# Two more pairs of output-projection tiles by seven block products, on one core

## What is computed

```python
u, gate = proj[..., :E_A], proj[..., E_A:]
pooled = multiscale_causal_pool(u)
y = jnp.einsum('bsgc,gcd->bsgd', pooled, w_grp_a[i]).reshape(b, s, E_A) * scale_a[i]
x = x + (y * jax.nn.silu(gate)) @ w_out_a[i]
...
kv_in = rmsnorm(x, norm_kv)
...
x = x + (merged * jax.nn.silu(gate)) @ w_out_b[i]
return rmsnorm(x, norm_f)
```

## Time and profile before

| | us |
|---|---|
| median of 3 runs | 2318.03 (2317.78 to 2319.93) |
| the profiled execution's own time | 2317.87 |
| its span in the trace | 2316.1 |
| PE busy in the span | 2299.1 |

### The profile page before, as it was taken

One profiled execution on the slowest core, in us unless ns is written; L12 is line 12 of the kernel. 1 busy time (PEld: TensorE's weight loads), 2 busy tenths in 40 slices (PEclk: granted clock), 3 DMA queues, 4 the chain that ended last, 5 costly groups with the idle time before them and its releaser, 6 DMA issues.

```text
span 2316.1 us, 31102 instructions
## 1 busy us (share of the span) xinstructions
PE 2299.1 (99%) x10665; PEld 1886.4 (81%) x10665; DVE 1824.8 (79%) x2349; ACT 1185.2 (51%) x1510; POOL 449.1 (19%) x878
## 2 busy tenths in 40 slices
PE   9999999999999999999999999999999999999998
PEld 6878788888878888888888888888888888888887
DVE  5888899999777676888688886666788768888764
ACT  3544546544574444555455565445655544444653
POOL 0001001334001211212100001112012145686310
PEclk9999999999999999999999999999999999999999
DMA  9996569999958887666666656666556676666564
GB/s 392 396 335 245 162 232 370 355 338 342 360 179 287 309 281 253 217 209 213 207 224 204 235 187 232 220 220 205 190 199 228 216 218 189 193 203 200 183 211 153
DMA packets 178821, 566.95 MB, mean 245 GB/s; under 512 B 30816, under 2 KB 35200, under 8 KB 178304
## 3 DMA queue, kind: packets, MB, share of 16 engines
q1 hardware_dynamic: 145584, 528.28, 66.4%
q0 software_dynamic: 27136, 23.91, 3.5%
q10 hardware_dynamic: 5968, 13.00, 1.6%
HBM read 537.01 MB, written 4.21 MB: 234 GB/s over the span
## 4 chain that ended last, share of the span: by engine, by line
PE 90%; DVE 4%; DMA 3%; issue 1%; ACT 1%; ACTq 0%; SPq 0%; DVEq 0%
PE acc L2903 25%; PE acc L2904 25%; PE acc L2910 25%; DMA raw<-in_wa_dram 2%; DVE lo L1701 1%; PE tb L3398 1%; PE tb L3405 1%; PE tb L3399 1%; PE acc L3405 1%; PE acc L3398 1%; PE acc L3399 1%; DMA start_raw<-in_wa_dram 1%; PE tb L3597 1%; DVE macc L1934 1%; PE tb L2990 1%
## 5 line engine op out<-in xcount | busy, mean ns | idle before, releaser
L897 ACT ACTIVATE hi<-raw 128x1024 fp32r<-128x1024 f32 (+2 forms) x808 | 825.2, 1031 | 768.5 <-PE acc L2910 428.0
L1701 DVE TENSOR_TENSOR lo<-raw,hi 128x1024 fp32r<-128x1024 f32 (+1 forms) x748 | 892.0, 1209 | 318.8 <-ACT hi L897 312.9
L2903 PE MATMUL acc<-hi,Hh 128*128 128x512 f32 x1816 | 714.0, 393 | 1.9 <-issue 1.5
L2904 PE MATMUL acc<-hi,Hl 128*128 128x512 f32 x1816 | 707.4, 390 | 0.0
L2910 PE MATMUL acc<-lo,Hh 128*128 128x512 f32 x1816 | 485.7, 389 | 0.0
L2903 PEld LDWEIGHTS acc<-hi,Hh 128*128 128x128 f32 x1816 | 341.0, 188 | 80.3 <-issue 8.2
L2910 PEld LDWEIGHTS acc<-lo,Hh 128*128 128x128 f32 x1816 | 340.9, 188 | 71.3
L2904 PEld LDWEIGHTS acc<-hi,Hl 128*128 128x128 f32 x1816 | 341.1, 188 | 69.2 <-issue 0.2
L2903 PE MATMUL acc<-hi,hbh 128*128 128x512 f32 x512 | 202.8, 396 | 0.0
L2904 PE MATMUL acc<-hi,hbl 128*128 128x512 f32 x512 | 199.6, 390 | 0.0
L803 POOL DMA_DIRECT2D tok<-sgt x176 | 85.9, 497 | 493.0 <-DVE sgt L1877 381.8
(11 more groups left out here) (496 smaller groups left out, 2917.5 us busy)
## 6 DMA issues: line engine op xcount, KB each, us to landing
raw<-in_wa_dram SPq DMA_DIRECT2D x680, 512.0 KB, 4.5
raw<-in_wb_dram SPq DMA_DIRECT2D x96, 512.0 KB, 4.5
late_raw<-in_wa_dram SPq DMA_DIRECT2D x90, 512.0 KB, 6.6
start_raw<-in_wa_dram SPq DMA_DIRECT2D x70, 512.0 KB, 7.8
raw<-in_wc_dram SPq DMA_DIRECT2D x64, 512.0 KB, 4.2
tok<-sgt POOLq DMA_DIRECT2D x416, 32.0 KB, 4.3
landed<-sgt POOLq DMA_DIRECT2D x192, 32.0 KB, 4.1
pt_landed<-att_parts POOLq DMA_DIRECT2D x192, 12.0 KB, 3.1
```

The lines of the kernel that those rows point to most:

```text
L897: act.activation(hi[:, s, n], w, ACT.Copy).then_inc(hi_ready, 1)
L1701: dve.tensor_tensor(lo[:, s, 0:n], raw[:, r, 0:n], hi[:, s, 0:n].bitcast(F32), ALU.subtract)\
L2903: pe.matmul(dst(tt), a, hi[:, s, w], start=first[tt] and i == 0, stop=False, skip_group_check=shared)
L2904: pe.matmul(dst(tt), b, hi[:, s, w], start=False, stop=False, skip_group_check=shared)
```

## The change

Both projections get one pair of tiles with two groups of sevens each.

- First projection, tiles 1 and 2: 20 ring places instead of 16. Tile 1's units 2, 3, tile 2's 2, 3, tile 1's 4, 5; the first group (unit 0 of both) at places 6 to 9; tile 2's unit 4; the second group (unit 1 of both) at 11 to 14; tile 1's last two; tile 2's last three. Before the last three PE waits for `sums_added`. Since all four banks of `tb` are used, DVE's `combine_out` has one step more than `combine_tiles`.
- Last projection, tiles 3 and 4: the order of the key-value pairs, with groups at places 3 to 6 and 8 to 11, and the last four units by halves as before.
- Tile 1's and tile 3's results are complete only after DVE's `add_to_first`.
- ACT's loop over three pooling groups is written out, since the third now has a `round_forms` in it.

```diff
 A_LOADS = 4 * 19 + 8 + 8 * 8 + 4 * 8 + 4 * 8 + FT * 16 + 4 * (FK // 2) + 4 * 20 + 3 * 32
-A_UNITS = A_LOADS + 2 * (2 * 8 + 2 * 4 + 2 * 3)
+A_UNITS = A_LOADS + 2 * (2 * 8 + 2 * 4 + 2 + 2 * 3)
...
+OUT_A0 = KV_AT[0] - 2 * 16 - 4
+OUT_SEVEN = {0: 6, 1: 11}
+OUT_PLACES = {0: (0, 2), 1: (0, 3), 2: (1, 2), 3: (1, 3), 4: (0, 4), 5: (0, 5), 10: (1, 4), 15: (0, 6), 16: (0, 7),
+              17: (1, 5), 18: (1, 6), 19: (1, 7)}
...
+LAST_PAIR = A_UNITS + B_UNITS + 4 * 8 + 2 * 8
+LAST_PAIR_SEVEN = {0: 3, 1: 8}
+LAST_PAIR_PLAIN = range(2, 8)
...
-            with c.loop(act, 3, unit=20, raw=20, u_turned=2) as g:
-                pooled_group(g + 1, last=g * MOVED + MOVED)
+            for g in range(1, 4):
+                if g == 3:
+                    split(2)
+                    round_forms(FORM_TILES + 1)
+                pooled_group(g, 8 if g < 3 else 6, last=g * MOVED)
...
-            split(7)
+            split_to(OUT_A0 + 17)
+            copy_shared(out_shared, OUT_A0 + 14, TT * OUT_TURN)
+            split_to(OUT_A0 + 20)
             y2_out(0)
-            split(8)
+            split_to(OUT_A0 + 24)
             y2_out(1)
...
             for i in range(3):
-                split(8)
+                if i < 2:
+                    split_to(LAST_PAIR - 4 + 8 * i)
+                else:
+                    split_to(LAST_PAIR + 14)
+                    copy_shared(gated_shared, LAST_PAIR + 11, TT * LAST_TURN)
+                    split_to(LAST_PAIR + 17)
...
-            for g in range(1, 4):
-                pooled_group(g)
...
+            pooled_group(1)
+            pooled_group(2)
+            chain(dve.tensor_tensor(out_slices[:], zh[:, 0:4, :].bitcast(F32), zl[:, 0:4, :].bitcast(F32), ALU.add))
+            add_forms(lambda f: out_forms[:, f], out_block)
+            split(4)
+            split_forms(FORM_TILES + 1)
+            pooled_group(3, 8 - 4)
+
+            def combine_out():
+
+                dve.wait_ge(unit_used, RING + OUT_A0 + 15)
+                dve.wait_ge(shared_copied, OUT_TURN + 1)
+                chain(dve.tensor_tensor(out_outer[:, 0, :], tb[:, 1, :], out_shared[:], ALU.add))
+                dve.tensor_tensor(out_inner[:], tb[:, 2, :], out_outer[:, 0, :], ALU.add)
+                chain(dve.tensor_tensor(out_outer[:, 0, :], tb[:, 3, :], out_outer[:, 0, :], ALU.add))
+                chain(dve.tensor_tensor(out_outer[:, 1, :], tb[:, 3, :], out_inner[:], ALU.add))
+                for b in range(1, 4):
+                    dve.sem_inc(tb_free[b], 1)
+                dve.tensor_tensor(acc[:, 2:4, :], acc[:, 2:4, :], out_outer[:], ALU.add).then_inc(sums_added, 1)
...
-            split(7)
+            split_to(OUT_A0 + 17)
+            combine_out()
+            split_to(OUT_A0 + 20)
+            dve.wait_ge(unit_used, RING + OUT_A0 + 17)
+            add_to_first((out_shared[:], out_inner[:]))
+            dve.wait_ge(first_summed, TT * (OUT_TURN + 1))
             y2_add(0)
             turn_blocks(head_major, y2_blocks, 0)
-            split(8)
+            split_to(OUT_A0 + 24)
             y2_add(1)
             dve.wait_ge(y2_moved, MOVED)
             turn_blocks(head_major, y2_blocks, 1)
...
             for i in range(3):
-                split(8)
-                tile_done()
...
+                else:
+                    split_to(LAST_PAIR + 14)
+                    combine_tiles(LAST_PAIR, LAST_TURN, out_outer)
+                    split_to(LAST_PAIR + 17)
+                    sum_first(LAST_PAIR, LAST_TURN, out_outer)
+                    dve.wait_ge(first_summed, TT * (LAST_TURN + 1))
...
-            tile(zh, zl, 0, 8, before={0: lambda: pe.wait_ge(z_split, 2), 4: lambda: pe.wait_ge(z_split, 3), 6: split_now}, after={1: last_group})
-            tile(zh, zl, 1, 8)
+            first_tiles = [open_tile(0)]
...
+                if (t, i) == (1, 5):
+                    pe.wait_ge(sums_added, OUT_TURN + 1)
...
-            for t in range(4):
-                if t == 0:
...
+            tile(Hh, Hl, 1, 8)
+            tiles_by_sevens(LAST_PAIR_PLAIN, LAST_PAIR_SEVEN, FORM_TILES + 3, by_halves=True)
```

More of the change, by code:

```diff
@@ L388, in two_blocks @@
         h_forms = sb("h_forms", [P, FORMS, 2, P], at=x_at)
-        block_sums = [sb(f"block_sums{i}", [P, 2, UNIT], at=at) for i, at in enumerate((x_at, h_at + 8 * KB, tok_at, free + 64 * KB))]
+        block_sums = [sb(f"block_sums{i}", [P, 2, UNIT], at=at) for i, at in enumerate((x_at, h_at + 8 * KB, tok_at, free + 48 * KB, free + 64 * KB))]
         gated_outer = sb("gated_outer", [P, 2, N], at=free + 2 * FK * T * 4)
@@ L1544, in _ @@
             split_to(KV_AT[0] + 14)
-            round_forms(FORM_TILES + 1)
+            round_forms(FORM_TILES + 2)
             for i in range(4):
@@ L3387, in _, with seven_products @@
             tile(Hh, Hl, 1, 8, before={0: lambda: pe.wait_ge(x_split, 7), 2: lambda: pe.wait_ge(x_split, 8)})
-            def seven_products(banks, plain, summed, first, last):
+            def seven_products(banks, plain, summed, first, last, joined=False):
                 x1, x5, x6, x7, c11, c12, c21 = banks
                 for part, groups in enumerate((((x1, plain(0, 0), 0, first, last), (c11, plain(1, 0), 1, False, False)),
-                                               ((c12, summed(3), 1, first, last),),
+                                               ((c12, summed(3), 1, first and not joined, last),),
                                                ((x5, summed(0), 0, first, last), (x7, summed(2), 1, first, last)),
@@ L3408, in _, with tiles_by_sevens @@
             halves = slice(0, P), slice(P, T)
-            def tiles_by_sevens(plain, sevens, form):
+            def tiles_by_sevens(plain, sevens, form, by_halves=False):
                 first, last = open_tile(0), plain[-1]
@@ L3428, in tiles_by_sevens @@
                 pe.wait_ge(sums_added, c.up("added"))
-                for i in plain:
+                for i in plain[:-RING] if by_halves else plain:
                     unit(second, Hh, Hl, 2 * i, 2, N, False, i == last, shared=True)
+                if by_halves:
+                    tile_by_halves(Hh, Hl, 1, last + 1, dst=second)
             for n in range(1, FT):
@@ L3567, in third_out @@
                 transpose_tok(0, tr_split)
-            tile(zh, zl, 0, 8, before={0: lambda: pe.wait_ge(z_split, 2), 4: lambda: pe.wait_ge(z_split, 3), 6: split_now}, after={1: last_group})
-            tile(zh, zl, 1, 8)
+            first_tiles = [open_tile(0)]
+            pe.wait_ge(z_split, 2)
+            at = 0
+            while at < 20:
+                if at in OUT_SEVEN.values():
+                    j = list(OUT_SEVEN.values()).index(at)
+                    if j == 0:
+                        for b in range(4):
+                            fill(b)
+                        pe.wait_ge(form_split, FORM_TILES + 2)
+                    seven_products((tb[:, 0, :], tb[:, 3, :], tb[:, 1, :], tb[:, 2, :], acc[:, 0, :], acc[:, 2, :], acc[:, 1, :]),
+                                   lambda e, tt: (zh[:, 2 * j + e, halves[tt]], zl[:, 2 * j + e, halves[tt]]),
+                                   lambda f: (formh[FORM_TILES + 1][:, f, j, :], forml[FORM_TILES + 1][:, f, j, :]), j == 0, j == 1, joined=True)
+                    at += 4
+                    continue
+                t, i = OUT_PLACES[at]
+                if (t, i) == (1, 2):
+                    first_tiles.append(open_tile(1))
+                if (t, i) == (0, 4):
+                    pe.wait_ge(z_split, 3)
+                if (t, i) == (0, 6):
+                    split_now()
+                if (t, i) == (1, 5):
+                    pe.wait_ge(sums_added, OUT_TURN + 1)
+                unit(first_tiles[t], zh, zl, 2 * i, 2, N, i == 2, (t, i) in ((0, 7), (1, 4), (1, 7)), shared=t == 1)
+                if at == 1:
+                    last_group()
+                at += 1
             tile(zh, zl, 0, 8)
@@ L3739, in _layout @@
         wa += [_units(w_in_a[:, g * N:(g + 1) * N]), _units(w_in_a[:, D + g * N:D + (g + 1) * N]), grp]
-    wa += [_units(a["w_out_a_2"][0])]
+    out_a = by_tile(a["w_out_a_2"][0])
+    places = {place: out_a[t][i:i + 1] for place, (t, i) in OUT_PLACES.items()}
+    places.update({place: np.stack([out_a[t][i] for t in range(2)]) for i, place in OUT_SEVEN.items()})
+    wa += [places[place] for place in sorted(places)] + out_a[2:]
     for n in range(4):
```

59 lines of the change are left out of this document (42 added, 17 removed).

## The result

| | before | after |
|---|---|---|
| median, us | 2318.61 (2317.70 to 2319.93, 12 runs) | 2323.72 (2322.71 to 2324.66, 12 runs) |
| profiled execution, us | 2317.87 | 2324.11 |
| its span, us | 2316.1 | 2322.4 |
| PE busy, us | 2299.1 | 2298.7 |

A forecast was written before the change was run, and what follows sets the result against it. PE was taken to bound the kernel: number of matmuls times their distance. -2.72 + 0.1 + 1.1 + 0.7 + 1.1 = +0.3 us against 2317.87 gave 2318.2, the median 0.16 higher: 2318.3; range 2315.2 to 2321.0.

The forecast's parts named there:

- The saved 2.72 us: Both projections: four groups of sevens save 12 matmuls at 0.2267 us each, 1.36 us at each projection.
- The forms: Both projections: extra slice sums and remainders on DVE and rounding on ACT fit in idle time; cost 0, at most 1 us.
- the groups' own sums: Both projections: DVE makes the second group's sums and remainders in time, with about 1.2 us margin; cost 0.
- Step 1: First projection, first wait for the sums: the longer combination nearly uses up PE's margin; 0 to 0.3 us, 0.1 taken.
- Step 2: First projection, tile 3's first unit: its rounding queues behind ACT's wait for tile 1; PE waits 1.1 us (0.7 to 1.6).
- Place 2: Last projection: PE waits 1.1 us for the third-last unit's remainder; with 1.36 saved, -0.3 us in sum.
- place 1: Behind the first projection's groups: 1.36 us saved against waits of 0.1, 1.1 and 0.7, +0.5 us in sum.
- a gap that is none of those listed: Sign in the profile after: any PE gap not forecast would show the prediction wrong in its completeness.
- The slower clock: Rival: TensorE's clock falls after a stall; 1 us stalls should leave it at 2.4 GHz; counted within the slower case, 0.05.
- Step 3: First projection, tile 3's fifth unit: its remainder queues behind GpSimd's moves and DVE's transposes; PE waits 0.7 us (0 to 1.3).

The follow-up runs named there:

- nowait: The changed kernel without PE's wait for banks 0 and 1 of `tb` at place 15; 2321.05 us.
- handover2: The kernel before with only the last projection's pair; ACT rounds two more units before squaring tile 3, DVE makes two remainders earlier; 2317.43 us.
- act_first: `nowait` with ACT rounding two units of the next tile before it takes tile 1; 2320.51 us.
- add_first: `handover1` with DVE adding tile 3 before the remainders of the second half of tile 1's blocks; 2319.01 us.
- early: The changed kernel, wait at place 15 kept, with DVE freeing bank 1 of `tb` after the combination's first step; 2320.86 us.
- handover1: `act_first` with DVE making two remainders before it waits for the moves of tile 1's blocks; 2317.87 us.
- later: The changed kernel with DVE freeing bank 1 of `tb` after the combination's third step instead of its fourth; 2323.15 us.
- best_wait: `handover1` with the reordering of `handover2` and the wait at place 15 kept; 2321.84 us.
- pair1: The changed kernel with the last projection as before the change; 2324.30 us.

## Why the prediction was wrong, point by point

**What held.** The saved 2.72 us: the groups run as forecast, 4.77 us without a gap, in both places. The forms and the groups' own sums: cost 0, no wait there in any kernel. Step 1, the sums at place 17: 0.18 us plus 0.1 of restart in `nowait`, forecast 0.1, within its bounds. Its chain was 0.35 us too short, though: the combination took 4.66 us against 4.31, because DVE is idle 0.69 us ahead of its last step, where the key-value pair has 0.24. Step 2, ACT at place 20: 1.14 us in `nowait`, forecast 1.1. Its terms behind the combination hold within 0.05 us; all of it lies 0.35 us later than chained, and PE, held up by 0.28 us at the sums, comes almost as much later. Place 2: 1.10 us and the restart, forecast 1.1, in the changed kernel itself, and `handover2` shows that it was the order that made it.

**The step that failed** is the first sentence on place 1: PE then has five plain units, "two before its wait for `sums_added`". The prediction took over from the key-value pairs that PE's first wait behind the groups is that one. In the code there is another, two places earlier, carried over unchanged from the old order. Its meaning changed, because it waits for a counter that the new groups move on. It costs 3.9 us of stall with its restart and 1.6 us of slower clock behind it, and no bound of the sum held either. The prediction named this kind of failure without looking for it, as a gap that is none of those listed. What would have found it was a list of all the waits of PE between the group's end and place 20, each with the value of its counter in the new program.

**The slower clock** was a rival, dismissed for stalls of 1 us. That holds: behind the gaps of 1.1 to 1.85 us of `nowait`, `act_first`, `add_first` and `early` the granted clock stayed at 1.00. The stall was 3.8 us, not 1, and there the 1.59 us come from. Given the stall, the rival was right.

**Step 3** had the right mechanism and too small a size: 1.29 us in `nowait` against 0.7, just at the upper bound of 1.3. The last move let DVE go on 16.45 us after `y2_add`'s start instead of 15.8, so 0.65 us later than chained. Its statement on what comes after was wrong, "after that ACT and DVE are where they were before relative to PE". They were not: the ring's loads were late behind it, and tile 3's addition came late enough to stop PE once more at tile 4 (1.15 us in the changed kernel, 0.77 in `nowait`) and some 0.4 us at the start of the key-value tiles. `act_first` still has 1.85 us in tile 3, 0.53 at tile 4 and the 0.4; `handover1`, which differs from it in two moved remainders alone, has none of them. In `nowait`, that is, without the wait at place 15, the forecast's sum becomes -2.72 + 0.28 + 1.14 + 1.29 + 0.77 + 0.4 + 1.2 = +2.4 us, and the medians say +2.4 (2321.05 against 2318.65).

**The size.** So of the 5.4 us between forecast and result, the line at place 15 has 2.7 (`nowait`), and the other 2.7 are step 3's longer wait (0.6), its echoes at tile 4 and behind (1.2), 0.3 at the sums and for restarts, and 0.6 of the starting point: the forecast counted from 2318.03, the median of three runs, and the twelve of the result have 2318.61. The range's upper end, 2321.0, is what the kernel without that line takes (2321.05), but by luck: it was added up from 1 us for the forms and longer waits at tile 3 and in the last tile, which did not come, and held nothing for tile 4 and the key-value tiles.

## What to carry to other kernels

When a change puts new work between a counter's increment and an old wait on that counter, read every kept wait again with its new value: a line carried over word for word can be the costliest part of the change. What an engine owes to others at a handover (here a tile to be taken, while four units of the ring wait behind it) should be split so that the feed of the bottleneck comes first; moving two remainders over one wait was worth 2.6 us here (`act_first` to `handover1`), while moving too much (`add_first`) made the next handover late. And a stall that covers others is not worth its length: the same wait cost 2.7 us in one kernel and 5.2 in another.

## What the runs showed of the hardware

The granted clock fell to 0.50 at PE's idle stretches of 3.1 us (`later`) and 3.8 us (the changed kernel, `best_wait`, `pair1`), and not at those of 1.75 to 1.85 us (`early`, `add_first`, `act_first`) or the shorter ones; between 1.85 and 3.1 us no run has one. Once low, it stayed so for 3.4 us in three of the four profiled executions and for 6.8 us in `pair1`, though PE had matmuls to do: each came 0.427 us after the last instead of 0.227. That cost 1.6 us in the first case and 2.7 us in the second. With the same stall the moment of the fall differed too: in `pair1` it lay 1.3 us before PE's restart, in the changed kernel 1.2 us behind it, where this window and the one shown above meet:

```profile
1601.00:1602.20 1.20, 1.16 (x5) 1.02 (x6) 0.63 (x1) 0.00 (x0) 0.00 (x0) 1.00 0.41 167
```

The Trainium skill, page "TensorE: Matmul & The Clock Gate", section "Wait — 56ns, not 53.3ns?", gives 426.7 ns from start to start at the low clock and 215.7 ns at the high one for 512 columns. The rows agree with the first (0.427) and not with the second (0.227).

Signals between two dependent steps of DVE go with idle time in its timeline as well. In the changed kernel three stand ahead of L2691, and DVE was idle 0.69 us there. Where two stand there, it was 0.24 (the key-value pair, `later`) and 0.25 (`early`), and in `early` the combination took 4.32 us instead of 4.66. Why the third costs more than the first two is open.
